# Neighbourhood attention: who evacuates q and k, and where the token's scale enters their head norm

## The reference, cut to what matters

```python
h = rms_norm(x, norm1_g)                  # one scale per token: 1/sqrt(mean(x*x) + EPS)
z = h @ w_in
a, gate, q, k, v = jnp.split(z, splits, axis=-1)
conv_out = conformer_conv(a, gate, dw_kernel, dw_bias, conv_ln_g, conv_ln_b)   # 31 taps
q = rms_norm(q.reshape(B, S, N_HEADS, HEAD_DIM), q_norm_g)     # per head of 64 channels
k = rms_norm(k.reshape(B, S, N_HEADS, HEAD_DIM), k_norm_g)
attn_out = neighbourhood_attention(q, k, v, rpb)               # 8 heads, 16 x 64 grid
```

## Time and profile before

| | |
|---|---|
| median of three runs | 2379.57 us |
| the profiled execution, as timed | 2379.88 us |
| its span, first to last instruction | 2378.1 us |
| PE busy | 2283.6 us (96%), mean granted clock 0.986 |
| DVE busy | 1603.1 us (67%) |
| ACT busy | 1094.1 us (46%) |
| POOL busy | 1165.9 us (49%) |

### The profile page before, as it was taken

How to read it: one execution, slowest core, us unless ns; L and a number is a source line. 1 busy time by engine, 2 the same in 40 slices (tenths; PEclk the granted TensorE clock), 3 DMA queues, 4 the chain that set the end, 5 groups by cost and what they waited for, 6 DMA issues and landing times. The chain is left out here.

```text
span 2378.1 us, 28950 instructions
## 1 busy us (share of the span) xinstructions
PE 2283.6 (96%) x10276; PEld 1755.2 (74%) x10276; DVE 1603.1 (67%) x1909; ACT 1094.1 (46%) x1776; POOL 1165.9 (49%) x832
## 2 busy tenths in 40 slices
PE   8989999989999999999999998997999999999999
PEld 6866656868888887887765565574788888888887
DVE  7889994596566667557746767549766656444587
ACT  5146665254444453223146666426666652222342
POOL 1000000568787877777511111142877777777732
PEclk9989999999999999999999998998999999999999
DMA  3211101313443429874200000212556677976312
GB/s 131 58 40 35 35 28 69 135 45 138 173 154 139 177 107 362 339 273 170 67 24 18 19 27 21 100 53 89 239 239 249 250 301 306 373 277 243 147 40 80
DMA packets 89165, 342.90 MB, mean 144 GB/s; under 512 B 22400, under 2 KB 23168, under 8 KB 76096
## 3 DMA queue, kind: packets, MB, share of 16 engines
q1 hardware_dynamic: 88368, 336.65, 37.6%
q10 hardware_dynamic: 656, 4.41, 0.5%
HBM read 224.16 MB, written 116.27 MB: 143 GB/s over the span
## 5 line engine op out<-in xcount | busy, mean ns | idle before, releaser
L1124 PE MATMUL ps<-operand,turn_weights 128*128 128x512 f32 x3192 | 735.5, 392 | 18.7 <-POOL turn_weights L730 5.3
L1124 PEld LDWEIGHTS ps<-operand,turn_weights 128*128 128x128 f32 x3192 | 599.3, 188 | 153.6 <-issue 15.0
L730 POOL TENSOR_TENSOR turn_weights<-turn_raw,turn_weights 128x512 fp32r<-128x512 f32 (+1 forms) x330 | 443.9, 1356 | 228.2 <-ACT turn_weights L1586 227.5
L1124 PE MATMUL ps<-hidden_operand,turn_weights 128*128 128x512 f32 x2268 | 517.5, 390 | 3.3 <-issue 1.5
L1124 PEld LDWEIGHTS ps<-hidden_operand,turn_weights 128*128 128x128 f32 x2268 | 424.8, 188 | 95.9 <-issue 6.0
L2804 DVE TENSOR_TENSOR branch_out<-ps,branch_out 128x1024 f32<-128x1024 f32 x172 | 210.5, 1224 | 201.2 <-PE ps L1124 200.2
L1586 ACT ACTIVATE turn_weights<-turn_raw 128x512 fp32r<-128x512 f32 (+1 forms) x330 | 204.9, 623 | 266.6 <-PE ps L1124 251.2
L690 POOL TENSOR_TENSOR weight_hi<-weight_raw,zero_col 128x1024 fp32r<-128x1024 f32 (+1 forms) x26 | 53.8, 2071 | 534.4 <-PE ps L1023 363.5
L844 PE MATMUL ps<-input_hi,weight_hi 128*128 128x512 f32 x592 | 196.4, 413 | 24.2 <-DVE input_lo L2368 9.9
L844 PE MATMUL ps<-input_lo,weight_hi 128*128 128x512 f32 x656 | 206.0, 396 | 0.0
L844 PE MATMUL ps<-input_hi,weight_lo 128*128 128x512 f32 x592 | 185.3, 395 | 0.0
(11 more groups left out here) (351 smaller groups left out, 3556.7 us busy)
## 6 DMA issues: line engine op xcount, KB each, us to landing
hidden_operand<-hidden_kept SPq DMA_DIRECT2D x91, 1024.0 KB, 8.0
hidden_kept<-hidden_parts SPq DMA_DIRECT2D x54, 1024.0 KB, 8.9
hidden_kept<-hidden_parts SPq DMA_DIRECT2D x27, 1536.0 KB, 6.1
turn_raw<-w_ff SPq DMA_DIRECT2D x40, 512.0 KB, 4.1
turn_raw<-w_mlp SPq DMA_DIRECT2D x32, 512.0 KB, 4.3
turn_raw<-w_mlpd SPq DMA_DIRECT2D x32, 512.0 KB, 4.5
turn_raw<-w_ffd SPq DMA_DIRECT2D x20, 512.0 KB, 4.5
weight_raw<-w_out SPq DMA_DIRECT2D x16, 512.0 KB, 3.7
```

The costliest lines, as they stand in the source:

```text
L730: pool_.tensor_tensor(place(p, 1), place(p, 1, WT) if raw is None else raw, bits(place(p, 0)), ALU.subtract).then_inc(s["st_lo"], 1)
L1124: ins = mm(PS[:, b, :], weights(p, w, k), tokens(p, a, k), start=(FRESH[p] and k == 0 and step == 0), stop=(k == n - 1 and step == 2), ski ...
```

## The change

ACT takes over the evacuation of q and k. It squares straight from the banks and then copies the raw tile, without the token's scale, into `work_a` or `work_b`; the copy frees the banks. DVE's eight evacuations of q and k go, those of v stay. The head's mean square is then that of the raw tile, so its EPS has to be scaled: once, at the start, DVE computes `E2` = EPS * (m + EPS) for every token from the banks with the mean square, ahead of `scale_from`, and PE adds the head mean of `E2` to each head mean by a second product into the same bank, ahead of the one of the squares. `head_guess` and `head_norm` leave their own EPS out. No operation's place in the order of an engine is changed otherwise.

```diff
+        E2 = at("eps_scaled", [P, T], R2 + 28672)
             def head_mean_square(i, b):
+                half = slice((i % 2) * H2, (i % 2 + 1) * H2)
+                if i == 0:
+                    pe.wait_ge(s["eps_scaled"], 1)
+                mm(PS[:, b, :], MEANH[:], E2[:, half], start=True, stop=False)
                 pe.wait_ge(s["qk_sq"], i // 2 + 1)
-                mm(PS[:, b, :], MEANH[:], (SQ, TC)[i // 2 % 2][:, (i % 2) * H2:(i % 2 + 1) * H2],
-                   start=True, stop=True).then_inc(s["qk_m"], 1)
+                mm(PS[:, b, :], MEANH[:], (SQ, TC)[i // 2 % 2][:, half], start=False, stop=True).then_inc(s["qk_m"], 1)
...
             def head_square(c, j):
-                act.wait_ge(s["bank_free"], U_QKV + 3 * c + j + 1)
+                raw = by_row(bank(0 if c else 2 * j))
+                if c:
+                    act.wait_ge(s["qk_lo"], 2 * c + j - 1)
+                else:
+                    act.wait_ge(s["w_split"], U_QKV + 2)
                 if j and c:
                     act.wait_ge(s["v_tr"], 2 * c)
-                act_.activation((SQ, TC)[j][:], (TA, TB)[j][:], ACT.Square).then_inc(s["qk_sq"], 1)
+                act.wait_ge(s["unit_done"], U_QKV + 3 * c + j + 1)
+                act_.activation(by_block((SQ, TC)[j][:]), raw, ACT.Square).then_inc(s["qk_sq"], 1)
+                copy(by_block((TA, TB)[j][:]), raw).then_inc(s["bank_free"], 1)
...
-                chain(act_.activation(y0, PS[:, b, :], ACT.Ln, bias=EPSC[:, 0:1]))
+                chain(act_.activation(y0, PS[:, b, :], ACT.Ln, bias=ZERO[:, 0:1]))
...
             weight_lo(2)
+            dve.wait_ge(s["ln_exp"], 2)
+            ts(by_block(E2[:]), by_row(bank(6)), EPS, EPS, ALU.add, ALU.mult).then_inc(s["eps_scaled"], 1)
+            dve.wait_ge(s["eps_scaled"], 1)
             scale_from(1)
...
-                stt(ps, ps, EPS, T2[:], ALU.add, ALU.mult).then_inc(s["qk_a"], 1)
+                tt(ps, ps, T2[:], ALU.mult).then_inc(s["qk_a"], 1)
...
-            evac(0, 0, 0)
...
-            evac(0, 1, 2)
...
-                    evac(c + 1, 1, 0)
...
-                if j == 1:
-                    evac(c + 1, 0, 0)
-                elif j == 2:
+                if j == 2:
```

More of the change, by code:

```diff
@@ L383, in program @@
             x_in2 x_in3 bt_masked split_hi split_lo sq_ready sq_added mean_done ln_exp scale_ready glu_sig
-            qk_sq qk_m qk_y0 qk_a qk_scaled qk_hi qk_lo v_tr v_ready neg_ready neg_out table_out
+            eps_scaled qk_sq qk_m qk_y0 qk_a qk_scaled qk_hi qk_lo v_tr v_ready neg_ready neg_out table_out
             bt_in0 bt_in1 bt_in2 bt_in3 scores_done scores_max probs_done probs_sum probs_scaled pt_done pt_sb pv_done
@@ L2440, in mix_lo, with v_evac @@
                 tt(INL[:, k, :], src, INH[:, k, :].bitcast(f32), ALU.subtract).then_inc(s["mix_lo"], 1)
[L2442 to L2445, removed]
+            def v_evac(c, b):
+                dve.wait_ge(s["unit_done"], U_QKV + 3 * c + 3)
+                tt(by_block(TC[:]), by_row(bank(b)), by_row(RS[:]), ALU.mult).then_inc(s["bank_free"], 1)
             def head_norm(i, b):
@@ L2499, in _ @@
             head_lo(0, 1)
-            evac(0, 2, 6)
+            v_evac(0, 6)
             weight_lo(U_QKV + 4)
@@ L2531, in first_part @@
                     head_lo(c + 1, 1)
-                    evac(c + 1, 2, 0)
+                    v_evac(c + 1, 0)
             def second_part(c, j):
-                if j == 1:
-                    evac(c + 1, 0, 0)
-                elif j == 2:
+                if j == 2:
                     conv(1)
```

## The result

The changed kernel takes 2405.6 us (median of four runs, 2399.1 to 2410.1) against 2378.4 us for the kernel before, run beside it: a ratio of 1.0107, 95% interval 1.0094 to 1.0121. It is slower by 27 us.

What follows compares the result with a forecast made beforehand. The prediction took PE's waits for the two banks to come free as the bound. Start 2.5, pair 0 1.5, q 4.9, k 11.4 and clock 8.7 summed to 29.0 us slower: 2408.6 us, range 2394 to 2414.

Steps and rivals of the forecast that it cites:

- What bounds the kernel: In each cycle, the path runs over the moment the two banks come free for PE; DVE's busy share is no help.
- Start: DVE's scaled-EPS operation ahead of `scale_from` delays PE's unit 3: +2.5 us, bounds 0 and 2.5 + 2.7 with clock lost.
- Pair 0: Second products of the q means and first k half delay DVE's head norm, low part and first scores: +1.5 us.
- q (column block 1): ACT's square and copy of next q, behind its exponentials, free the banks later for piece 8: +1.64 us, three times, +4.9.
- k (column block 4): Later square and copy of next k delay piece 16, then mean m2 adds 0.94: 3.63, 4.13 and 3.63, +11.4 us.
- PE's clock: Low clock behind PE's longer waits at pieces 8 and 16: +5.5 us and +3.2 us, +8.7 us in all.
- The sum: Start, pair 0, q, k and clock together: 2.5 + 1.5 + 4.9 + 11.4 + 8.7 = 29.0 us, giving 2408.6 us.
- Rival (a): PE's clock holds behind the longer waits, since one wait's length alone doesn't decide it: +20.3, 2399.9 us; chance 0.35.
- Rival (b): DVE's stream of taps bounds the cycle and is relieved, if ACT frees banks no later than DVE: 2372.3 us; chance 0.07.
- Rival (c): Cycles come out even, DVE's 2.4 us per cycle paying; only start and pair 0 remain: +4.0, 2383.6 us; chance 0.05.

Runs made afterwards that it cites:

- e4_ahead: Changed kernel, with ACT's square and copy of next pair's q moved ahead of column block 1's exponentials, k's to the end of column block 3: 2383.7 us.
- e5_copy_first: Changed kernel, but ACT copies the two banks out first and then squares the tile: 2395.1 us.
- e2_no_second: Changed kernel without the second product of each head mean, so the head norms lack their EPS: 2400.6 us.
- e3_dve_evac: Changed kernel, but DVE copies raw q and k out at its old places and ACT squares the tile; scaled EPS and second products stay: 2387.5 us.
- e7_busy_wait: Changed kernel, with PE running 12 extra unused products ahead of piece 8 and 9 ahead of piece 16 while it waits: 2396.2 us.
- f1_before_busy: Kernel before the change, with PE running 6 extra unused products ahead of piece 8 and 4 ahead of piece 16: 2375.5 us.
- e6_ahead_late: Changed kernel with the moves of e4_ahead, and the scaled EPS made by ACT from the token scale in idle time ahead of pair 0: 2380.0 us.
- f2_ahead_one_pass: e6_ahead_late with both operands of the second product rounded so that PE takes it in one pass instead of float32: 2372.5 us.

## Why the prediction came out as it did

The forecast was 2408.6 us, 3.0 us above the measured median, which lies within the range. In the profiled executions, on which it was summed, 29.0 was forecast; the last mark moved by 29.3, of which 1.2 lies ahead of the change, so 28.1. The mechanism held. Several terms were off, in both directions, so that the sum came this close is partly luck.

- **What bounds the kernel.** Right: PE's waits for the banks, not DVE's busy share. e4_ahead shows it, where nothing but the place of the squares and copies in ACT's order moved, and e5_copy_first, where the banks alone came free 0.9 us sooner and the cycles fell by 6.0.
- **Start.** The 2.5 us were right to the tenth (3.72 less 1.22). The clock behind that gap was left to the bound of +2.7, and that was wrong: the q unit of pair 0 ends 5.2 us later, 1.2 + 2.5 + 1.5 of low clock. It was no certain loss either: e2_no_second, the same program up to there, kept its clock (last section). The granted clock in the changed kernel:

```profile
51.00:55.00 4.00, 3.95 (x11) 3.17 (x12) 3.93 (x4) 1.06 (x1) 0.00 (x0) 0.59 0.50 134
```

- **Pair 0.** +1.5 was forecast; from the first read of the q unit's banks to the first scores it grew from 33.80 to 35.24 us, +1.44. With DVE's evacuations back (e3_dve_evac) it is 35.24 too, so they gave nothing there, as said.
- **q (column block 1).** 1.64 a cycle was forecast. At full clock (e7_busy_wait against f1_before_busy, by DVE's first score operation of each column block) it is 1.4 to 1.6. The copy took 1.01 us where 1.06 was taken.
- **k (column block 4).** 3.63, 4.13 and 3.63 were forecast, 11.4 in all; at full clock it is 4.2, 3.7 and 3.7, 11.6 in all. Up to the head norm of the third guess it is 3.4 in each. Behind that, DVE's low part of q waits 0.77, 0.30 and 0.29 us for ACT's high part, which it does not do in the kernel before, and the step did not have that. The slack of the third guess does not part the cycles: DVE's wait of 1.20 in cycle 1 is gone when the waits are filled, so it came with the low clock behind piece 16. First f1_before_busy, the end of that guess and its head norm, then e7_busy_wait, the low part of q in cycle 0:

```profile
256.73 0.63 ACT L1675 ACTIVATE guess_squared<-work_c 128x512 f32<-128x512 f32 x1
...
257.94 0.70 DVE L2459 SCALAR_TENSOR_TENSOR ps<-ps,guess_squared 128x512 f32<-128x512 f32 x1
...
217.50 1.23 DVE L2480 TENSOR_TENSOR q_lo<-work_a,q_hi 128x1024 fp32r<-128x1024 f32 x1 [0.77 <-ACT q_hi L1597]
```

- **PE's clock.** This is the term that was mis-sized: 8.7 forecast, 6.4 measured, and laid to the wrong places. No run shows the 8.7: it was added up on the premise that each of the six waits costs the clock, being longer than the 2.97 us of the earlier trace rows, behind which the earlier trace rows have 0.50. But behind piece 16 of cycle 2, after 3.06 us, the changed kernel had 1.00. The forecast had 1.6, 2.7 and 4.3 for the cycles, the runs show 2.8, 2.0 and 1.6. By place: behind piece 8 of cycles 1 and 2 it took the price of the kernel before's cycle 0, 2.73 each, and the new loss is 1.6 and 1.5. Behind piece 16 it had 1.6 in cycle 0, and that is 2.8; nothing in cycle 1, and that is 0.4; 1.6 in cycle 2, which kept its full clock (0.1). "All six new waits are longer than the one that surely cost the clock" was no argument: 3.06 us of wait went three ways.
- **The sum.** 16.3 for q and k were forecast and 16.2 measured; the clock's 2.3 too much and the start's 1.5 too little nearly cancel. That is luck. In the busy times DVE fell by 7.2 us where 8.5 was forecast, ACT rose by 6.6 (8) and PE by 19.7 (14).
- **Rival (a)**, the clock holds, was wrong by the 6.4 us and the start's 1.5, though the wait's length alone does not decide it, as it said.
- **Rival (b)**, DVE relieved, fails at the condition it names: the banks came free later, not sooner. Where it is met, the cost is gone: e6_ahead_late is even with the kernel before (0.9999), and f2_ahead_one_pass, with cheaper products, is faster (0.9970).
- **Rival (c)** had DVE's 2.4 us a cycle pay for the rest. DVE stands idle for the guess instead.

## What to carry to other kernels

When an evacuation moves to an idler engine, ask what stands in front of it in that engine's own order, and when the bank then comes free; the engine's busy share says nothing about that (here DVE was busy 7.2 us less, and the kernel took 27 us more). A matmul added ahead of a wait is cheap only as long as the wait is there: it cost half its time with DVE's evacuations (1.6 to 1.8 of 3.4 us a cycle), and with the banks free in time most of what PE saved on it came back (2.0 of 2.5 us in cycles 1 and 2). A lengthened wait of PE is to be charged for the clock behind it as a range (here 0.1 to 2.8 us a place), and filling the wait with products that nobody uses measures it (10.4 us of the changed kernel's cycles, 4.0 of the kernel before's).

## What the runs showed of the hardware

The length of the wait alone does not say whether the granted clock falls. A wait of 1.55 us ahead of piece 8 of cycle 0 (e4_ahead) was followed by two matmuls in 1.19 us, one of 3.06 us ahead of piece 16 of cycle 2 (the changed kernel) by two in 0.70. What PE did ahead of them differs (in e4_ahead another wait of 2.27 us ended 2.4 us before piece 8), and no run here isolates it. At the start the same program differs from itself: e2_no_second and e4_ahead are alike up to unit 3, wait 3.21 us in front of it and begin it with two matmuls in 0.70 us; then e2_no_second keeps its clock, and e4_ahead, whose unit 3 starts at 49.70 us against 50.91, does not (e2, then e4):

```profile
50.00:54.00 4.00, 3.09 (x14) 2.57 (x15) 3.93 (x5) 1.16 (x2) 0.00 (x0) 1.00 0.47 133
...
50.00:54.00 4.00, 4.00 (x13) 3.17 (x12) 3.92 (x4) 1.06 (x1) 0.00 (x0) 0.63 0.47 134
```

ACT's read of two banks with the order of the tokens changed took 1.00 to 1.03 us, square or copy, against 1.22 for DVE's evacuation: the reordering cost ACT nothing visible beside its plain read of 1.02.
